# A hybrid decoder layer: the prompt's output products as three fp32r products each, and the sample selection's end moved behind h2

## What is computed

```
h = rms_norm(x, norm1_g)
u, q, k, v, iq, ik, iw = project(h, ...)
ya = pool_mix(u, ...) * pool_scale              # 512 channels, 4 groups
yb = sparse_attention(q, k, v, iq, ik, iw)      # 4 heads x 128, top-k keys by an indexer
x = x + concatenate([ya, yb]) @ w_o             # 1024 x 1024
h2 = rms_norm(x, norm2_g)
q = h2 @ w_pq                                   # 2048 columns = 16 chunks of 128
s = q . sub_keys; top 16 of 16 x 16 sums        # 8 heads
a = gelu(h2 . expert_u[e]); x = x + sum(g * a * expert_v[e])
```

## Time and profile before

| | |
|---|---|
| median of 3 runs | 981.35 us (981.3 to 982.72) |
| profiled execution | 981.55 us, its span 980.1 us |
| granted TensorE clock | 1.0 of full speed, all through |
| PE, PEld busy | 98%, 85% of the span |
| DVE, ACT, POOL busy | 79%, 57%, 45% |
| DMA | 221 MB, mean 226 GB/s |

### The profile page before, as it was taken

The page is one execution under the profiler, slowest core; times in us unless marked ns, Lnnn a source line. Parts: engine busy times, 40 slices in busy tenths (PEclk is TensorE's granted clock), DMA queues, the critical chain, the costliest instruction groups (busy, mean ns, idle before and its releaser), DMA issues.

```text
span 980.1 us, 19215 instructions
## 1 busy us (share of the span) xinstructions
PE 958.2 (98%) x6440; PEld 835.3 (85%) x6440; DVE 777.5 (79%) x1805; ACT 558.6 (57%) x1092; POOL 438.6 (45%) x328
## 2 busy tenths in 40 slices
PE   5999999999999999999999999999999999999998
PEld 2347879899999999999999998888888888888887
DVE  2569987269999948999999976777888878788873
ACT  2023354454445559999999975654555555555552
POOL 4643465145788776776777770011212211131200
PEclk9999999999999999999999999999999999999999
DMA  9635748668855554444445456797888888888872
GB/s 330 149 109 160 238 139 308 209 226 316 280 176 175 180 185 150 152 161 160 150 155 165 151 173 217 257 337 283 300 300 305 299 279 296 303 304 303 291 263 94
DMA packets 75424, 221.24 MB, mean 226 GB/s; under 512 B 11301, under 2 KB 23725, under 8 KB 74964
## 3 DMA queue, kind: packets, MB, share of 16 engines
q1 hardware_dynamic: 60812, 179.12, 53.7%
q0 software_dynamic: 12800, 40.36, 13.3%
q10 hardware_dynamic: 1744, 0.92, 0.4%
HBM read 217.41 MB, written 3.14 MB: 225 GB/s over the span
## 4 chain that ended last, share of the span: by engine, by line
PE 86%; DVE 4%; DMA 4%; ACTq 2%; ACT 2%; issue 2%; SPq 0%; DVEq 0%
PE psum L1123 33%; PE psum L1059 22%; PE psum L1060 12%; PE psum L1071 3%; PE psum L1055 3%; PE psum L603 3%; PE psum L872 2%; ACTq L402 1%; PE psum L873 1%; DMA w_raw<-expert_v 1%; DMA rows_in<-expert_u,eidx 1%; PE psum L581 1%; DMA w_raw<-expert_ut 1%; DVE work L1825 1%; PE psum L887 1%
## 5 line engine op out<-in xcount | busy, mean ns | idle before, releaser
L1630 POOL TENSOR_TENSOR w_lo<-w_raw,w_hi 128x1024 fp32r<-128x1024 f32 x116 | 279.1, 2410 | 124.1 <-ACT w_hi L1170 123.9
L1059 PE MATMUL psum<-h_split,w_hi 128*128 128x256 f32 x1792 | 327.0, 284 | 1.3 <-issue 1.3
L1060 PE MATMUL psum<-h_split,w_lo 128*128 128x256 f32 x1024 | 289.4, 283 | 0.0
L1059 PEld LDWEIGHTS psum<-h_split,w_hi 128*128 128x128 f32 x1792 | 279.2, 192 | 2.6 <-issue 1.4
L1170 ACT ACTIVATE w_hi<-w_raw 128x1024 fp32r<-128x1024 f32 x214 | 224.9, 1051 | 39.4 <-DMA w_raw<-expert_ut 27.6
L1060 PEld LDWEIGHTS psum<-h_split,w_lo 128*128 128x128 f32 x1024 | 196.1, 191 | 0.0
L2145 DVE TENSOR_TENSOR w_lo<-w_raw,w_hi 128x1024 fp32r<-128x1024 f32 x98 | 120.5, 1229 | 54.7 <-ACT w_hi L1170 54.4
L1123 PE MATMUL psum<-w_hi,ag_hi 128*128 128x512 f32 x512 | 158.2, 390 | 0.4 <-DVE ag_lo L2152 0.4
L1123 PE MATMUL psum<-w_hi,ag_lo 128*128 128x512 f32 x512 | 158.0, 389 | 0.0
L1170 ACT ACTIVATE ag_hi<-store 128x256 fp32r<-128x256 f32 x128 | 53.2, 417 | 152.5 <-PE psum L1123 152.4
L1123 PEld LDWEIGHTS psum<-w_hi,ag_hi 128*128 128x128 f32 x512 | 95.8, 188 | 20.6 <-ACT w_hi L1170 0.8
(11 more groups left out here) (347 smaller groups left out, 1485.0 us busy)
## 6 DMA issues: line engine op xcount, KB each, us to landing
w_raw<-expert_ut SPq DMA_DIRECT2D x128, 512.0 KB
w_raw<-expert_v SPq DMA_DIRECT2D x86, 512.0 KB
raw_more<-expert_v SPq DMA_DIRECT2D x42, 512.0 KB, 4.8
w_slice<-w_pq_cols SPq DMA_DIRECT2D x32, 512.0 KB, 5.3
w_most<-w_in_blocks SPq DMA_DIRECT2D x8, 699.0 KB, 11.3
w_slice<-w_o_half SPq DMA_DIRECT2D x8, 512.0 KB, 4.7
v_cache<-cache_v POOLq DMA_DIRECT2D x64, 64.0 KB, 3.7
w_o_sb<-w_o_half SPq DMA_DIRECT2D x8, 512.0 KB, 6.1
```

The lines of the kernel that those rows point to most:

```text
L1059: pe.matmul(out, w_hi[:, s, c, :], h_split[:, c, a], start=(c == 0 and a == 0), stop=False)
L1060: mm = pe.matmul(out, w_lo[:, s, c, :], h_split[:, c, 0], start=False, stop=(c == KC - 1), skip_group_check=wide)
L1630: pool.tensor_tensor(w_lo[:, s], w_raw[:, s], w_hi[:, s].bitcast(F32), ALU.subtract).then_inc(S["w_lo_ready"], 1)
```

## The change

- The output products of the prompt run as three fp32r products each, like the retrieval chunks: `high_o` on ScalarE and `low_o` on GpSimd split each slice of `w_o`; the concatenated rows are split too, into `cat_hi_p`, `cat_hi_a` (ScalarE) and `cat_lo` (GpSimd for the pooled half, `low_yb` on VectorE for the heads).
- The sample tokens' part of the concatenation gets its own tile, `cat_s`.
- `prompt_logits(0)` moves from before the pooling mixer's products to behind them.
- `join`, `order` and `cut` move behind h2 and its low parts, between the low parts of chunks 3 to 5; `tally` and `admit` follow, and what depends on them moves two chunks later. `rq(2)` comes before `rs(0)`.
- ScalarE's copy of the sample logits is parted: the four new keys' columns go to `few_s`, the rest is copied after `cut`.
- SyncE takes 24 of the 64 V pages, in between the slices; 8 K pages move behind slices 1 to 3. The first two expert slices don't wait any more.

```diff
@@ SyncE
-            k_loads(8, 24)
+            k_loads(8, 16)
             sp.wait_ge(S["zp_done"], 8)
             sp.wait_ge(S["idx_summed"], 2)
             for q in range(EARLY, 4):
                 load_slice(q)
-            k_loads(32, K_SP - 32)
-            for q in range(4, 12):
+            k_loads(24, K_SP - 24)
+            load_slice(4)
+            sp.wait_ge(S["log_p_psum"], 2)
+            v_loads(0, 4)
+            for i in range(1, 4):
+                load_slice(4 + i)
+                v_loads(4 * i, 4)
+            for q in range(8, 12):
                 load_slice(q)
+            v_loads(16, V_SP - 16)
...
@@ TensorE
+            def wo_half(q, a, cat_hi, cat_part, first):
+                c = CHUNKS[2 * (q % 4) + a]
+                hi, lo = (w.rearrange("p (a k) j -> p a k j", a=2)[:, a] for w in (o_high(q), q_lo[:, q % SLICES]))
+                for k in range(4):
+                    if first and q == 0 and a == 1:
+                        pe.wait_ge(S["pool_copied"], NG + k + 1)
+                    pe.matmul(wo_bank(c), hi[:, k, :], cat_hi[:, k, :], start=(first and k == 0 and c % 2 == 0),
+                              stop=False, skip_group_check=True)
+                    pe.matmul(wo_bank(c), lo[:, k, :], cat_hi[:, k, :], start=False, stop=False, skip_group_check=True)
+                for k in range(4):
+                    if first:
+                        pe.wait_ge(S["cat_lo_p"], k // 2 + 1)
+                    else:
+                        pe.wait_ge(S["cat_lo_a"], 2)
+                    mm = pe.matmul(wo_bank(c), hi[:, k, :], cat_lo[:, cat_part + k, :], start=False,
+                                   stop=(not first and k == 3), skip_group_check=True)
+                return mm
...
-            prompt_logits(0)
             pe.wait_ge(S["late_in"], 16 * len(late_loads))
...
-            wo_first(0, (1, 0), ready=True)
+            prompt_logits(0)
+            wo_first(0, (1, 0))
             prompt_logits(1)
...
@@ ScalarE
+            def high_o(q):
+                act.wait_ge(w_slice_in[q % SLICES], 16 * (q // SLICES + 1))
+                if q in (5, 6):
+                    act.wait_ge(S["wo_half"], q - 2)
+                if q == 7:
+                    act.wait_ge(S["wo_psum"], 2)
+                copy(o_high(q), w_slice[:, q % SLICES]).then_inc(S["q_hi_ready"], 1)
+
+            high_o(0)
+            high_o(1)
             for g in range(NG):
                 act.wait_ge(S["pool_psum"], g + 1)
                 copy(dT[:, g, :], psum[:, 4 + (g + 1) % 4, 0:NT]).then_inc(S["pool_copied"], 1)
...
+            high_q(4)
+            copy_q(2)
             copy_log(0)
+            high_q(5)
+            copy_q(3)
             copy_log(1)
...
@@ GpSimd
+            def low_o(q):
+                pool.wait_ge(S["q_hi_ready"], q + 1)
+                pool.tensor_tensor(q_lo[:, q % SLICES], w_slice[:, q % SLICES], o_high(q).bitcast(F32), ALU.subtract
+                                   ).then_inc(S["q_lo_pool"], 1)
+            low_o(0)
+            low_o(1)
+            for g in range(0, NG, 2):
+                pool.wait_ge(S["pool_copied"], NG + g + 2)
+                pool.tensor_tensor(cat_lo[:, g:g + 2, :], cat_p[:, g:g + 2, :], cat_hi_p[:, g:g + 2, :].bitcast(F32),
+                                   ALU.subtract).then_inc(S["cat_lo_p"], 1)
+            low_o(2)
+            low_o(3)
             pool.wait_ge(S["log_p_psum"], 2)
+            v_loads(V_OVER, 4)
+            for q in range(4, KC):
+                low_o(q)
...
@@ VectorE
-            rounds(ROUNDS - done[0])
+            rounds(4)
+            low_yb(0)
+            rounds(4)
+            low_yb(1)
+            rounds(2)
             add_wo(0)
-            join(0)
-            for i in range(1, 5):
+            for i in range(1, KC):
                 add_wo(i)
-                order(2 * i - 2)
-                order(2 * i - 1)
-            add_wo(5)
-            cut(0)
-            add_wo(6)
-            add_wo(7)
+                if done[0] < ROUNDS and i < KC - 1:
+                    rounds(1)
...
+            join(0)
+            order(0)
+            order(1)
+            low_q(3)
+            for stage in range(2, 5):
+                order(stage)
+            low_q(4)
+            for stage in range(5, STAGES):
+                order(stage)
+            cut(0)
+            low_q(5)
             tally(0)
-            low_q(3)
+            low_q(6)
             admit(0)
-            for r in range(4, 7):
-                low_q(r)
...
+            low_q(7)
             bar(0)
-            low_q(7)
             max_s(0)
             low_q(8)
             bar(1)
             low_q(9)
```

214 lines of the change are left out of this document (117 added, 97 removed).

## The result

The changed kernel takes 994.18 us (median of 4 runs, 993.68 to 996.55), the kernel before beside it 981.86 us: a ratio of 1.0126 (95% interval 1.0111 to 1.0142), 1.3% slower. I had forecast 990.4, slower, within 981.0 to 994.0. The direction and the place were right. The size was 3.8 us short, just outside the range.

The account below looks back on a forecast made before the run. TensorE, busy 958.2 of 980.1 us, was taken as the bound. Waits outweighing the 5.0 us gain summed to a 9.9 us shift, less 0.8, so 990.4 us was forecast, range 981.0 to 994.0.

Parts of the forecast that it names:

- The gain on PE: Prompt output products: 64 fp32 products, 28.0 us, become 192 fp32r ones, 23.0 us; gain 5.0 us if operands are there.
- Step 1: First prompt logits: near 100.1, VectorE's maximum 4.4 us late, second mask at 106.8, PE idle about 4 us.
- the lock: Shared SBUF port: a GpSimd subtraction blocks VectorE; priced at 0 to 2.9 us at h2.
- Step 2: Last weight slices: SyncE's queue is last, slice 7 requested at 127.7, products end at 137.8; path through the mask 134.5.
- Steps 3 to 5: Norm, chunk 4's low part, cut and copies: h2 at 142.5, slice 12 requested at 152.7, chunk 5 at 165.5.
- step 4: Chunk 4's low part: ready at 158.7 by SyncE's order, slice 12 landing in 3.7, later than VectorE's chain by 1 to 4.
- Step 6: Chunks 5 to 9: VectorE alternates low parts and selection, 18.5 us instead of 15.2; chunk 9 at 184.0, then 0.8 more.
- the sum: Whole kernel: shift of 9.9 us, less 0.8, gives 9.1; by itself 988.5 to 992.5, chance 0.45.
- the 0.8 us that I took off for a later stage: Unnamed later stage: might give back 0.8 us, estimated as the size of one wait of the trace.
- The gain arrives: Products end near 128, selection fits into existing waits, 5.0 and up to 2 us saved: 975.5 us; chance 0.16.
- SyncE is not last: Four-page calls cost well under 4.3 us, only VectorE's chain is left, products at 134.5: 986.5 us; chance 0.24.
- The lock on top: GpSimd holds VectorE at h2 and masks, 2.9 + 1, V pages slow slices 12 and 13: 993.5 us; chance 0.10.

Follow-up runs that it names:

- logits_early: Changed kernel with the first logits again right behind the score sums, ahead of the pooling mixer; 993.45 us, ratio 1.0155 to the kernel before.
- h2_alone: Changed kernel with GpSimd's low part of chunk 2 held until VectorE has written h2; 994.45 us, ratio 1.0159 to the kernel before.
- pages_behind_12: Changed kernel with SyncE's call for eight V pages behind the output rows and slices 12 and 13; 997.31 us, ratio 1.0182.
- quiet_norm_2: Changed kernel with first logits, V pages, splits, low parts and copies reordered together, joins behind h2; 982.48 us, ratio 1.0009 to the kernel before.

## Why the prediction was right, and where it was wrong

**The gain on PE** was sized right: 24 matmuls take 2.9 us. It was spent in waits, as forecast.

**Step 1** held: maximum at 99.37 (forecast 100.1), lateness 3.7 to 4.4 us. I had priced the lock only at h2, and at the masks only in a rival. It came at the mask too, 2.0 us.

**Step 2** gave the right time, 137.7 against 137.8, for the wrong reason, so by luck. A round of SyncE took 4.1 to 4.5 us, not 4.9, and slice 7 did not hold TensorE. The chain through the mask, which I had at 134.5, was last: the mask was ready 1.2 us later than I had it (108.0, the lock), and half clock in the second logits cost 1.6 us (3.9 instead of 2.3). Together that is 137.3; the 1.34 us before the low part of the heads I had counted (1.6). In logits_early, with this chain shorter, SyncE's limit showed at once, 1.68 us; I had the order of the two limits reversed and both close.

**Steps 3 to 5** held within 0.7 us: h2 at 142.16, slice 12 requested at 152.03, chunk 5 at 166.24. The lock took its 1.3 us at h2, but the later releaser that I had named decided: h2_alone, without it, starts chunk 5 no earlier. In step 4 an earlier request (0.7) and a landing of 5.0 us instead of 3.7 offset each other in part; in pages_behind_12, without the same eight pages ahead of it, the landing took 3.6.

**Step 6 and the sum** failed. I priced the waits and put what the clock does behind them at nothing, without a reason. The waits were right (2.86 before chunk 9, forecast 2.7), and at full clock so were the stretches from chunk to chunk, all within 0.3 us (the table of the section on the clock). But chunk 5 took 1.3 us longer than in the kernel before (4.25 - 2.97) and chunk 9 1.5 (4.46 - 2.97), at half clock. The waits that this hid, among them the 0.8 us that I had counted for the key scores behind the exponential (0.56 at full clock), leave a net price of 1.4 us. This makes the shift at the first expert unit 11.8, not 9.9: of the 1.9 us between them 0.7 was there when chunk 5 started, 1.4 is the clock, and the rest came out 0.2 shorter than counted. And the 0.8 us that I took off for a later stage was never earned: from the first expert unit to the end the changed kernel is 0.7 us longer. 1.9 + 0.8 + 0.7 is the whole 3.4 us by which the span was missed; 0.4 more lie outside the span (1.82 us around it instead of 1.45). Where the 0.7 come from, no experiment was made to tell.

**Rivals.** The gain arrives: wrong for this kernel. Another order around it takes 6.5 us off A (quiet_norm_2, 40.5 against 47.0), but the best order ends level with the kernel before. SyncE is not last: true for the products, wrong for chunk 4. The lock on top: it came, 1.3 us at h2 and 1.2 to 2.0 at the mask, and the landing of slice 12 was slow; but taking the lock off alone moved the first expert unit by 0.2 us (mask) and chunk 5 by nothing (h2). That this branch, at 993.5, came nearest is luck: it holds nothing of the clock.

## What to carry to other kernels

Price a wait of TensorE with what runs behind it: between the score sums and the first expert unit of these traces, every unfilled wait of 3 us or more, and eleven of the fifteen from 2.0 to 2.9 us, had half clock at its end or within 2 us behind it. In the changed kernel the work behind took 1.3 to 1.6 us longer each time; what of it arrives depends on the next wait, here about half. A cheaper form of an operation that adds splits on ScalarE, subtractions on GpSimd and steps on VectorE is paid in the queues of those engines, so count these first; here 5.0 us saved met a serial chain that was already tight on three of them. When several queues are late by similar amounts, undoing one shows nothing, and only moving them together tells what the change is worth.
